# A two-layer decoder trunk with its layer loop written out, an earlier first half of the output, and three steps moved within their queues

## The reference

```python
for each of 2 layers:
    h = x + 0.5 * swiglu(rms(x), ffn1_wi, ffn1_wo)        # 1024 -> 2 x 2816 -> 1024
    n = rms(h); z = n @ w_in                              # one projection for all mixers and gates
    A = swish(layer_norm(causal_conv31(glu(z_a)))) @ conv_out
    B = (u * (tril(W_s) v + b)) @ sgu_out                 # chunks of 128, 4 groups
    C = nsa(q, kv, gates) @ nsa_out                       # 8 heads: compressed, selected, window
    h = h + (sig(gA)*A + sig(gB)*B + sig(gC)*C) @ w_out
    h = h + cross_attention(rms(h), rms(mem))             # 4 heads, 256 memory tokens
    x = h + 0.5 * swiglu(rms(h), ffn2_wi, ffn2_wo)
```

## Time and profile before

| what | value |
|---|---|
| median of 3 runs | 2733.23 us (2732.05 to 2734.7) |
| the profiled execution's own time | 2736.34 us |
| its span, first to last instruction | 2734.6 us |
| mean granted clock of PE | 0.993 of full speed |
| PE busy | 2669.5 us, 98% |
| POOL busy | 1228.0 us, 45% |
| DVE busy | 1205.8 us, 44% |
| ACT busy | 1114.9 us, 41% |
| DMA | 244.70 MB, mean 89 GB/s |

### The profile page before, as it was taken

One profiled execution on the slowest core, in us unless ns is written; L12 is line 12 of the kernel. 1 busy time (PEld: TensorE's weight loads), 2 busy tenths in 40 slices (PEclk: granted clock), 3 DMA queues, 4 the chain that ended last, 5 costly groups with the idle time before them and its releaser, 6 DMA issues.

```text
span 2734.6 us, 39624 instructions
## 1 busy us (share of the span) xinstructions
PE 2669.5 (98%) x13132; PEld 2141.2 (78%) x13132; DVE 1205.8 (44%) x1852; ACT 1114.9 (41%) x1682; POOL 1228.0 (45%) x616
## 2 busy tenths in 40 slices
PE   7999999989999999999999999999999999899998
PEld 6888888766678867888888888887667788688887
DVE  5222248777534643121341212677765364521224
ACT  5322242446644454232352222424576445542223
POOL 4444456662235414444444444567522354244443
PEclk9999999999999999999999999999999999999999
DMA  4335433212224313333233353432122342133332
GB/s 120 106 94 116 112 97 93 69 52 58 55 76 114 106 45 103 97 97 95 85 109 100 92 132 90 110 78 67 50 55 63 85 124 85 55 107 97 96 100 93
DMA packets 495745, 244.70 MB, mean 89 GB/s; under 512 B 49528, under 2 KB 493282, under 8 KB 495586
## 3 DMA queue, kind: packets, MB, share of 16 engines
q1 hardware_dynamic: 494816, 242.42, 32.0%
q10 hardware_dynamic: 770, 0.26, 0.0%
HBM read 240.51 MB, written 2.10 MB: 89 GB/s over the span
## 4 chain that ended last, share of the span: by engine, by line
issue 44%; PE 27%; POOL 21%; POOLq 7%; DVEq 0%; DVE 0%; ACT 0%
POOL wL L577 20%; PE pg L628 9%; PE pg L634 9%; PE pg L631 9%; POOLq L604 4%; POOLq L606 3%; POOL wsn L602 1%; POOLq L576 1%; POOLq L582 0%; DVEq L1601 0%; POOL convb L605 0%; DVE sacc L1606 0%; DVE big L2215 0%; ACT wH L1152 0%; PE pA L643 0%
## 5 line engine op out<-in xcount | busy, mean ns | idle before, releaser
L577 POOL TENSOR_TENSOR wL<-raw,wH 128x1024 fp32r<-128x1024 f32 (+1 forms) x472 | 1085.6, 2301 | 1474.6 <-ACT wH L1152 1471.3
L628 PE MATMUL pg<-gxH,wH 128*128 128x512 f32 (+1 forms) x2448 | 961.7, 393 | 6.9 <-POOL wL L577 4.5
L634 PE MATMUL pg<-gxH,wL 128*128 128x512 f32 (+1 forms) x2448 | 950.6, 388 | 0.0
L631 PE MATMUL pg<-gxL,wH 128*128 128x512 f32 (+1 forms) x2448 | 945.2, 386 | 0.0
L1152 ACT ACTIVATE wH<-raw 128x1024 fp32r<-128x1024 f32 (+1 forms) x474 | 476.5, 1006 | 534.4 <-PE pg L634 380.0
L628 PEld LDWEIGHTS pg<-gxH,wH 128*128 128x128 f32 x2448 | 461.8, 189 | 115.9 <-issue 24.3
L631 PEld LDWEIGHTS pg<-gxL,wH 128*128 128x128 f32 x2448 | 462.0, 189 | 93.7 <-issue 6.9
L634 PEld LDWEIGHTS pg<-gxH,wL 128*128 128x128 f32 x2448 | 461.9, 189 | 93.3 <-issue 3.9
L634 PE MATMUL pg<-hH,wL 128*128 128x512 f32 x992 | 392.0, 395 | 0.0
L628 PE MATMUL pg<-hH,wH 128*128 128x512 f32 x992 | 389.8, 393 | 0.3 <-POOL wL L577 0.3
L631 PE MATMUL pg<-hL,wH 128*128 128x512 f32 x992 | 389.8, 393 | 0.0
(11 more groups left out here) (230 smaller groups left out, 2232.0 us busy)
## 6 DMA issues: line engine op xcount, KB each, us to landing
raw<-in_ffn_wi SPq DMA_DIRECT2D x356, 256.0 KB, 3.1
raw<-in_w_in SPq DMA_DIRECT2D x200, 256.0 KB, 3.2
raw<-in_ffn_wo SPq DMA_DIRECT2D x128, 256.0 KB, 3.0
raw<-in_ffn_wo SPq DMA_DIRECT2D x64, 192.0 KB, 2.6
raw<-in_xkv SPq DMA_DIRECT2D x32, 256.0 KB, 3.1
raw<-in_w_out SPq DMA_DIRECT2D x32, 256.0 KB, 3.1
raw<-in_sgu_out SPq DMA_DIRECT2D x32, 128.0 KB, 2.2
raw<-in_conv_out SPq DMA_DIRECT2D x32, 128.0 KB, 2.3
```

The costliest lines, as they stand in the source:

```text
L577: pool.tensor_tensor(wL[:, s % 4, 0:n, :], raw[:, s % 2, 0:n, :], wH[:, s % 4, 0:n, :].bitcast(F32), ALU.subtract)\
L628: mm(o, wH[:, s, k, :], rh(k), start=(k == 0), stop=False)
L631: mm(o, wH[:, s, k, :], rl(k), start=False, stop=False)
L634: last = mm(o, wL[:, s, k, :], rh(k), start=False, stop=(k == kt - 1))
```

## The change

- **Layers.** The loop over the two layers is a loop of Python on all five engines, so each layer's instructions are written out. The loops in the feed-forwards stay.
- **Output.** In the last feed-forward of layer 2, after the sixth of the last 8 output units, PE turns tiles 0 to 3 (16 transposes into `pA`), ACT copies them and SP stores four halves. At the end only tiles 4 to 7 are left, in four banks. The norm after the last layer and the two surplus weight units are gone.
- **Convolution weights.** They are no longer loaded and turned at the start but per layer: 4 DMAs ahead of the 14 small ones, one transpose before unit `U_CONV`, one copy on DVE. The other parameters are turned after the fifth tile of x.
- **Statistics.** `stat(l, 2)` goes from between two units into unit `U_KV + 4`, after its sixth product.
- **Gates.** The tanh of the attention's gates goes behind `ahead(U_QP2)` and `v_out(1)` on ACT, their transposes from p = 4 to p = 7 on PE, behind the third `v_turned` in bank `pT`, and their use on DVE behind `mixed(0)`. `mixed` uses buffer `sil` in place of `hb`.
- **First steps.** DVE's `normed(l, 7)` goes from before step 1 to the end of step 2 in place of four taps; two taps more stand before `weigh` in steps 1 to 3; statistic "q2" goes from step 2 to step 3, with its root on ACT.
- **Lead.** In the second feed-forward ACT's weight copies are made one unit earlier (`lead` = 1), and the first of these stands before `root(l, 15)`.

```diff
-        pall = sb("pall", [P, L + 1, NPAR])
+        pall = sb("pall", [P, L + 1, NP_ROWS])
+        cwt = sb("cwt", [P, P])
...
-        EXTRA = {2: "q2", 4: "mean", 6: "var", 10: "q3"}
-        EXTRA_AT = {2: 3, 4: 4, 6: 5, 10: 3}
+        EXTRA = {3: "q2", 4: "mean", 6: "var", 10: "q3"}
+        EXTRA_AT = {3: 4, 4: 4, 6: 5, 10: 3}
...
-        small = sig("small", 16 * 14)
+        small = sig("small", 16 * 18)
...
-        FIN = (fin_act, fin_act, fin_act, fin_dve, fin_act, fin_dve, fin_act, fin_dve)
+        FIN = (fin_act, fin_act, fin_dve, fin_act)
...
+                for j in range(4):
+                    load_small(cwt[j * CONV_W:(j + 1) * CONV_W, :],
+                               conv_w[l, :, j * P:(j + 1) * P])
...
-            with sp.Fori(0, L) as l:
+            for l in range(L):
...
-            for u in range(2):
-                unit(L, u, 0, cols_of(ffn1_wi[0], u * P))
-            for n in range(2 * TT):
-                a, cols = n // 2, slice(n % 2 * T, (n % 2 + 1) * T)
-                sp.wait_ge(FIN[n], fin_count(n))
-                sp.dma_start(out[0, a * P:(a + 1) * P, cols], xnat[:, a, cols]).then_inc(stored, 16)
+            sp.wait_ge(fin0_cp, 1)
+            for hf in range(2):
+                for a in range(TT):
+                    cols = slice(hf * T, (hf + 1) * T)
+                    if hf:
+                        sp.wait_ge(FIN[a], fin_count(a))
+                    sp.dma_start(out[0, a * P:(a + 1) * P, cols], xnat[:, a, cols])\
+                      .then_inc(stored, 16)
             sp.wait_ge(stored, 16 * 2 * TT)
...
                     for m in range(KD):
                         unit(l, u + m, 0, n, lambda k: hH[:, k, :], lambda k: hL[:, k, :],
                              before=hid if m == 0 else None)
+                        if f == 1 and l == L - 1 and ch == len(CH) - 1 and m == 5:
+                            pe.wait_ge(evac, risen(evac, l, u + 4))
+                            for a in range(TT):
+                                for k in range(4):
+                                    last = turn(pA[:, a, k * P:(k + 1) * P],
+                                                xT[:, k, a * P:(a + 1) * P])
+                            last.then_inc(fin0_tr, 1)
...
-                if k == 5:
+                if k == 4:
                     pe.wait_ge(pro_par, 16 * (11 + 8))
                     for l in range(L):
                         last = turn(pT[:, l * P:l * P + NP_ROWS], ctab[0:NP_ROWS, l, :], NP_ROWS)
                     last.then_inc(pro_tr, 1)
-            pe.wait_ge(pro_cw, 16 * 4)
             for l in range(L):
-                last = turn(pA[:, 0, l * P:l * P + 4 * CONV_W],
-                            ctab[0:4 * CONV_W, L + l, :], 4 * CONV_W)
-            last.then_inc(pro_tr, 1)
-
-            with pe.Fori(0, L) as l:
                 ffn(l, 0, 0, 0, 0)
...
+                pe.wait_ge(small, risen(small, l, 16 * 18))
+                turn(pA[:, 0, 0:4 * CONV_W], cwt[0:4 * CONV_W, :], 4 * CONV_W).then_inc(cw_tr, 1)
                 unit(l, U_CONV, 0, KD, gH, gL, before=norm_ready(l, 1))
                 unit(l, U_CONV + 1, 0, KD, gH, gL)
 
                 unit(l, U_CONV + 2, 0, KD, gH, gL, between=within(6, lambda: stat(l, 1, ones)))
-                pe.wait_ge(small, risen(small, l, 224))
...
                     unit(l, U_KV + j, 0, KD, gH, gL)
-                stat(l, 2, bdon)
-                unit(l, U_KV + 4, 0, KD, gH, gL)
+                unit(l, U_KV + 4, 0, KD, gH, gL, between=within(6, lambda: stat(l, 2, bdon)))
                 v_rows(0)
                 unit(l, U_KV + 5, 0, KD, gH, gL)
                 stat(l, 3, bdon)
...
                 def gates_turned():
 
-                    pe.wait_ge(sg_cp, risen(sg_cp, l, 2))
+                    pe.wait_ge(sg_cp, risen(sg_cp, l, 3))
...
-                    elif c == 2:
+                    elif c == 3:
                         pe.wait_ge(t_free, risen(t_free, l, 4))
                     else:
                         pe.wait_ge(sg_cp, risen(sg_cp, l, c))
...
-                    if p == 4:
+                    if p == 7:
                         gates_turned()
...
             for a in range(TT):
-                for hf in range(2):
-                    n = 2 * a + hf
-                    if n >= 4:
-                        pe.wait_ge(FIN[n - 4], fin_count(n - 4))
-                    for k in range(4):
-                        last = turn(pg[:, n % 4, k * P:(k + 1) * P],
-                                    xT[:, 4 * hf + k, a * P:(a + 1) * P])
-                    last.then_inc(fin_tr, 1)
+                for k in range(4):
+                    last = turn(pg[:, a, k * P:(k + 1) * P], xT[:, 4 + k, a * P:(a + 1) * P])
+                last.then_inc(fin_tr, 1)
...
-                if u + 3 < U + 2:
+                if u + 3 < (U + 2 if l < L - 1 else U):
...
                     with act.Fori(0, n // 2) as i:
                         for c in range(2):
-                            ahead(l, u + 2 * c, i)
+                            ahead(l, u + 2 * c + lead, i)
 
                             act.wait_ge(evac, risen(evac, l, u + 2 * c + 1 + 4 * i))
                             act.activation(sil, tb[:, 0, :], ACT.Silu).then_inc(silu, 1)
-                            ahead(l, u + 2 * c + 1, i)
...
                     if ch == len(CH) - 1 and last_norm:
-                        norm(l, *last_norm, u)
+                        norm(l, *last_norm, u, lead=lead)
                     else:
                         for m in range(KD):
-                            ahead(l, u + m)
+                            ahead(l, u + m + lead)
+                        if lead and ch == len(CH) - 1:
+                            act.wait_ge(fin0_tr, risen(fin0_tr, l, 1))
+                            for a in range(TT):
+                                last = copy(xnat[:, a, 0:T], pA[:, a, :])
+                            last.then_inc(fin0_cp, 1)
...
-            for j in range(4):
-                act.dma_start(ctab[j * CONV_W:(j + 1) * CONV_W, L:2 * L, :],
-                              conv_w[:, :, j * P:(j + 1) * P].rearrange("l k c -> k l c"))\
-                   .then_inc(pro_cw, 16)
...
-            with act.Fori(0, L) as l:
+            for l in range(L):
...
                 v_out(0)
+                ahead(l, U_QP2)
+                v_out(1)
                 act.wait_ge(ng_in, risen(ng_in, l, 1))
                 act.activation(hb, sr, ACT.Tanh, scale=0.5).then_inc(ng_sig, 1)
-                ahead(l, U_QP2)
-                v_out(1)
                 ahead(l, U_QP2 + 1)
                 v_out(2)
...
-                    if i in (2, 6, 10):
+                    if i in (3, 6, 10):
                         act.wait_ge(st_out, risen(st_out, l, STEP[EXTRA[i]] + 1))
                         act.activation(rv[:, :], rv[:, :], ACT.Sqrt).then_inc(mid_rt, 1)
...
                 norm(l, 3, G_F2, gx_tile, U_XO, True)
+                ahead(l, U_F2)
                 root(l, 15, rstd, 1.0 / D)
                 act.wait_ge(par_in, risen(par_in, l, 2))
-                ffn(l, U_F2, (4, G_F1, gx_tile))
...
-                dve.tensor_copy(par[:, :], pall[:, bass.ds(n, 1), :]
+                dve.tensor_copy(par[:, 0:NP_ROWS], pall[:, bass.ds(n, 1), :]
...
             for l in range(1, L):
-                dve.tensor_copy(pall[:, l, 0:NP_ROWS], pT[:, l * P:l * P + NP_ROWS])
-                dve.tensor_copy(pall[:, l, NP_ROWS:NPAR],
-                                pA[:, 0, l * P:l * P + 4 * CONV_W])
+                dve.tensor_copy(pall[:, l, :], pT[:, l * P:l * P + NP_ROWS])
...
-            with dve.Fori(0, L) as l:
+            for l in range(L):
...
+                dve.wait_ge(cw_tr, risen(cw_tr, l, 1))
+                dve.tensor_copy(par[:, NP_ROWS:NPAR], pA[:, 0, 0:4 * CONV_W])
                 root_of(l, 1, rstd)
...
                 def mixed(c):
                     dve.wait_ge(sg_mm, risen(sg_mm, l, c + 1))
-                    t = (hb, sr)[c % 2]
+                    t = (sil, sr)[c % 2]
...
                 maxes_c(0)
+                mixed(0)
+                scaled(qT[:, 2, :], l, U_QP2)
                 dve.wait_ge(ng_tr, risen(ng_tr, l, 1))
                 TS(gates[:, :, :], pT[:, :].rearrange("p (a c) -> p a c", a=4)[:, :, 0:NG], 0.5,
                    0.5, ALU.mult, ALU.add)
@@ -1956,8 +1961,6 @@
 
                 cmp0 = gates[:, 0, 0:NG:3]
                 TS(cmp0, cmp0, valid[:, 0:1], None, ALU.mult).then_inc(t_free, 1)
-                mixed(0)
-                scaled(qT[:, 2, :], l, U_QP2)
                 maxes(0, 0)
...
                 weigh_c(0)
-                normed(l, 7, qT[:, 1, :], g8[:, 1:2])
-                dve.drain().then_inc(q_ok, 1)
...
-                    if i in (2, 10):
+                    if 1 <= i <= 3:
+                        conv(2)
+                    if i == 10:
                         middle_out(EXTRA[i])
                     if i < NS:
                         weigh(i)
```

(15 more changed lines are left out.)

32 lines of the change are left out of this document (16 added, 16 removed).

## The result

Changed kernel: 2718.6 us (five runs, 2717.8 to 2722.1). Beside it on the same chip the kernel before took 2733.4. The ratio is 0.9948 (0.9937 to 0.9958): faster, but 1.6 us above the top of the range. The profile is of a run of 2718.6 us with a span of 2716.9; the one of before has 2734.6, so 17.7 us between the spans are to be found.

What follows compares the result with a forecast made beforehand. PE, busy 98% of the span, was taken to bound the kernel, other engines mattering by what they release. Terms summed to -26.5 us: 2736.34 to 2709.8, predicted as 2706.7 because the median is 3.1 lower; range 2697 to 2717.

Steps and rivals of the forecast that it cites:

- Scores of step 1: Before step 1's maxima: moving DVE's reciprocal and product removes PE's waits of 2.23 and 2.22 us and clock loss, -9.5 us.
- steps 1 to 3: Attention steps: later probabilities +2.9, statistic "q2" +1.7, table load and root leaving ACT -2.4; sum +2.2 us.
- Gates: Attention gates: reordering removes PE's waits of 2.74 and 2.75 us and their clock loss, less 0.8; -7.8 us.
- the waits move: Rival: DVE's moved work meets POOL, step 3 waits 3 us a layer and the clock drops; +7, 2713.7 us, chance 0.2.
- shorter dispatch: Rival: without register work ACT and DVE answer sooner and remaining waits for ACT shrink by half; 2700 us, chance 0.13.
- Statistic: Statistic moved into the unit: PE's 1.33 us wait for DVE's squares is covered by six products; -2.7 us.
- Opening: Opening of the second feed-forward: earlier weight copy removes PE's waits of 2.12 and 2.14 us; -4.3 us.
- End: Kernel end: last store issue 4.1 us earlier, 16 turns moved into PE's stream cost 2.0; -2.1 us.
- The lead's cost: Later second feed-forward: copies wait for the unit just finished, adding at most 1 us to a 10 us chain; zero.
- The small loads: Rival: convolution-weight DMA issues ahead of the small loads stall PE 2.2 us a layer; 2711.1 us, chance 0.1.
- Start: Kernel start: four DMA issues leave ACT's queue, held for 5.25 us; about half comes through, -2.5 us.
- layer loop: Loops over the layers written out: one jump per engine and register work removed; -0.3 us.

Runs made afterwards that it cites:

- gates_alone: Kernel before with only the gates edit (turned at piece 7 instead of 4, DVE's first token mix and one scaling ahead): 2728.6 us, ratio 0.9985.
- filled_in_gaps: Changed kernel with 15 of DVE's taps made earlier where DVE stood idle, the 7 left laid into step 3's idle gaps: 2700.1 us, ratio 0.9878.
- filled_late: Changed kernel with 15 of DVE's taps made earlier, the 7 left in one block at the end of step 3: 2714.6 us, ratio 0.9936.

## Why the prediction was wrong

*What bounds the kernel.* Right for the feed-forwards, too narrow for the steps. "The others matter by what they release" was said, but DVE's share was then read over the whole span (44%). In the stretch it is 71 us of 95, one after the other, with maxima and weights for PE behind taps that could have stood elsewhere.

*Scores of step 1, "all of it goes: -9.5", and steps 1 to 3, "+2.2".* This is the failed step: +6.25 in place of -7.3. The waits of 2.23 and 2.22 us at step 1 were taken for the price of one piece of work in the wrong place; they were the lateness of DVE's whole queue. Without POOL's taps they were gone, and behind step 1 the two kernels then differed by 0.1 and 1.8 us, so the -7.3 did not appear there either. Three things were wrong in the working.
- The rows. The four taps of the earlier trace rows are not those that the edit replaced. They stand in step 1, behind its squares. The replaced ones stand at the end of step 2 and took 3.23 us in both layers, so 5.19 us was never to be had back:

```profile
610.83 3.23 DVE L1737 SCALAR_TENSOR_TENSOR convb<-convb,par 128x512 f32<-128x512 f32 x4
...
1961.47 3.23 DVE L1737 SCALAR_TENSOR_TENSOR convb<-convb,par 128x512 f32<-128x512 f32 x4
```

- The price of a tap. I left every tap at its old duration, though the groups of step 1 were going to stand at 572 to 592 us, where POOL has hardly a pause. They took 6.99 us instead of 4.70 and 7.19 instead of 3.23, and all 21 taps from step 1 to the mean 26.4 us instead of 21.2 in layer 1. The Trainium skill (SBUF — State Buffer, SBUF: two separate sides) gives the rule that I cited and then left out of the sum: a DVE instruction with two SBUF inputs and a GpSimd instruction that reads SBUF lock each other out for a whole instruction. The trace agrees: 1600 ns a tap beside POOL's taps, 907 without them. By the rule as I had costed it the sum was 2711.5, inside my range, and still 7 us short.
- The order removed a shield. The reciprocal of 3.35 us in the earlier trace rows takes one input. It lasted 3.35 us beside a POOL that was busy 3.73 us of the 4 from 582 to 586, as elsewhere beside an idle one. It filled DVE's time while POOL was busy, and the taps came later. The change put the taps first and the reciprocal at 602.5 us, when POOL had nothing of its tile left. This part is read from the timelines; no run tests it by itself.

*Gates, -7.8.* In their place they gave 7.3. In the total the edit alone gave 4.2: DVE comes to step 1 four microseconds earlier, with the same taps left and POOL as far behind as before. I had costed each wait as its own, though the next ones down the queue hung on the same engine.

*Rival "the waits move".* The right mechanism, chance 0.2, priced at +7 in all. Its signs came as written: waits over 2 us at step 3 with a lower clock. There were three such waits in layer 1 and two in layer 2, the last one in each at step 3 and the others in step 2. It lost against what was called a cover: that the opening's wait of 2.12 us had left the clock alone.

*Rival "shorter dispatch".* The 2.9 us that writing out the loops gave beyond the forecast go its way, but no trace shows its mechanism.

*Statistic.* Right: 2.9 for 2.7. *Opening* and *in-stream turns*: the `wL` waits fell from 4.8 to 0.3 us as said; the stage as a whole gave 4.4 for 2.35, but it differs as much between executions: gates_alone, which edits nothing there, has 1108.9 us from the mean of layer 1 to the turned mixer weights of layer 2, the kernel before 1113.5. So the size of this stage's gain is not shown. *End.* 4.7 for 4.1. The lead's cost of "zero, hidden by the four banks" held in time (the longest wait for `hL` is 0.8 us), though DVE's operations there took 2.2 us instead of 0.8. The small loads stalled nothing. *Start* and *layer loop* were undervalued, by about 2.4 and 3 us. These errors were on the cautious side, and they hid part of the large one.

The single terms don't add to the total exactly: 8.2 (loops and weights), 4.2 (gates), 2.9 (statistic) and 9.1 (the last two stages, which may hold a part of what the loops gave), minus 4.1 for the steps, make 20.3 against the 14.8 of the medians and 17.7 of the spans. What is left stays open; one stage alone differs by 4.6 us between executions, as said.

## What to carry to other kernels

Before a wait is counted as a gain, cut the trace at the next place where the same two engines meet, and look at how busy the late engine is up to there: a wait removed inside such a stretch mostly reappears at its end. Fillers belong where their engine waits for PE, never in a block ahead of what PE waits for, and vector work with two SBUF inputs not beside a busy GpSimd. When work is swapped in DVE's queue, price it by what POOL does at its new time, not by its row in the old place.

## What the runs showed that was not expected

- POOL's own taps are dear: leaving out 30 of them a layer, none of which PE waits for directly, took 14.7 us off the kernel before and 10.5 off the changed one.
- DVE operations that POOL slows can also cost next to nothing: 88 of them in the two second feed-forwards went from 0.8 to 2.2 us each, with 1.5 us of waits in PE.
- Accumulators in PSUM escape it: 14 taps with one SBUF input and one from PSUM took 10.33 us, 0.74 each, though a subtraction of POOL lies in them (filled_in_gaps):

```profile
468.53 10.33 DVE L1740 SCALAR_TENSOR_TENSOR pA<-convb,par,pA 128x512 f32<-128x512 f32 x14
...
475.94 2.40 POOL L585 TENSOR_TENSOR wL<-raw,wH 128x1024 fp32r<-128x1024 f32 x1 [8.48 <-ACT wH L1156]
```

- Even POOL's subtractions for the weight units show in a group of taps: three of the last seven took 2.40 us with POOL idle (0.80 each, as in the groups of four of 3.23 us), the other four 4.45 us with two subtractions reaching into them (filled_in_gaps), and all seven 7.71 us with one of 2.91 us (filled_late).
